# Page tiles regrouped as quarters of four pages, scales turned by VectorE, late pages gathered by GpSimd, weights and values one slot earlier

## What is computed

```python
def _decompress(c_kv, w_ukv, g_kn):
    kv = jnp.einsum('btc,chd->bthd', c_kv, w_ukv)
    return _rmsnorm(kv[..., :NOPE], g_kn), kv[..., NOPE:]

def _attn_partial(qn, qp, kn, kp, v, mask):
    s = (jnp.einsum('bqhd,bkhd->bhqk', qn, kn) + jnp.einsum('bqhr,bkr->bhqk', qp, kp)).astype(jnp.float32) * SCALE
...
    m = jnp.max(s, axis=-1)
    e = jnp.exp(s - m[..., None])
    return m, jnp.sum(e, axis=-1), jnp.einsum('bhqk,bkhd->bhqd', e, v.astype(jnp.float32))

    def step(carry, phys):
        c_blk = cache_ckv[layer, phys]
        kp_blk = cache_kpe[layer, phys]
        kn_blk, v_blk = _decompress(c_blk, w_ukv, g_kn)
        return _merge(carry, _attn_partial(qn, qp, kn_blk, kp_blk, v_blk, None)), None
```

## Time and profile before

| | us |
|---|---|
| median of 3 runs (lowest, highest) | 1275.35 (1275.25, 1277.68) |
| the profiled execution | 1276.86 |
| its span, first to last instruction | 1275.1 |
| TensorE busy | 1202.1 |
| VectorE busy | 732.2 |
| ScalarE busy | 426.5 |
| GpSimd busy | 257.4 |

### The profile page before, as it was taken

The page is one execution under the profiler, slowest core; times in us unless marked ns, Lnnn a source line. Parts: engine busy times, 40 slices in busy tenths (PEclk is TensorE's granted clock), DMA queues, the critical chain, the costliest instruction groups (busy, mean ns, idle before and its releaser), DMA issues. The chain is left out here.

```text
span 1275.1 us, 23690 instructions
## 1 busy us (share of the span) xinstructions
PE 1202.1 (94%) x8783; PEld 661.3 (52%) x8783; DVE 732.2 (57%) x1801; ACT 426.5 (33%) x1041; POOL 257.4 (20%) x294
## 2 busy tenths in 40 slices
PE   6999999989999999999989988999999999989898
PEld 3545677745565565655434445555444444454343
DVE  4000437955667666774768787888676667430331
ACT  3000354323343333342444343333444444210310
POOL 0000134711011121234412340001323232000000
PEclk9999999999999999997999999999999999999999
DMA  6413112123232222351453226532576544101000
GB/s 219 168 55 87 35 33 67 53 59 80 66 81 67 76 73 77 84 115 42 124 143 88 76 74 171 168 80 74 153 184 172 139 122 123 50 1 38 17 21 33
DMA packets 205236, 114.45 MB, mean 90 GB/s; under 512 B 152977, under 2 KB 196433, under 8 KB 204994
## 3 DMA queue, kind: packets, MB, share of 16 engines
q1 hardware_dynamic: 198482, 96.56, 27.7%
q0 software_dynamic: 4352, 10.49, 3.3%
q10 hardware_dynamic: 2288, 5.89, 1.3%
HBM read 75.79 MB, written 4.07 MB: 63 GB/s over the span
## 5 line engine op out<-in xcount | busy, mean ns | idle before, releaser
L563 PE MATMUL PS<-wk,c_T 128*128 128x512 f32 x1024 | 494.5, 612 | 13.5 <-DVE c_T L673 12.4
L563 PEld LDWEIGHTS PS<-wk,c_T 128*128 128x128 f32 x1024 | 180.3, 193 | 207.8 <-issue 162.8
L686 DVE TENSOR_REDUCE ssq<-PS 128x8 f32<-128x512 f32 x256 | 176.3, 689 | 169.7 <-ACT PS L609 156.8
L609 ACT ACTIVATE PS<-PS 128x512 f32<-128x512 f32 x256 | 150.3, 587 | 271.8 <-PE PS L563 245.0
L1557 PE MATMUL PS<-xnT,w_ring 128*128 128x276 f32 x416 | 101.0, 400 | 0.0
L1395 PE MATMUL PS<-w_ring,xnT 128*128 128x424 f32 x256 | 96.4, 534 | 0.9 <-DVE xnT L1041 0.9
L673 DVE STREAM_TRANSPOSE c_T<-blocks 128x512 f32<-128x512 f32 x126 | 88.3, 701 | 3.7 <-DMA blocks<-c_ring 3.2
L1557 PEld LDWEIGHTS PS<-xnT,w_ring 128*128 128x128 f32 x416 | 77.8, 190 | 20.6 <-issue 4.1
L489 POOL DMA_INDIRECT c_ring<-in_cache_ckv,token_rows x48 | 45.3, 944 | 182.1 <-PE PS L547 174.8
L480 POOL DMA_INDIRECT r_ring<-in_cache_kpe,group_rows x64 | 62.0, 969 | 92.3 <-DVE r_T L681 68.0
L1395 PEld LDWEIGHTS PS<-w_ring,xnT 128*128 128x128 f32 x256 | 48.8, 194 | 45.5 <-issue 45.4
(11 more groups left out here) (535 smaller groups left out, 1725.3 us busy)
## 6 DMA issues: line engine op xcount, KB each, us to landing
blocks<-c_ring SPq DMA_DIRECT2D x504, 64.0 KB
c_ring<-in_cache_ckv SPq DMA_DIRECT2D x208, 128.0 KB, 2.2
w_ring<-in_w_in SPq DMA_DIRECT2D x4, 1696.0 KB, 12.4
w_ring<-in_w_in SPq DMA_DIRECT2D x9, 512.0 KB, 5.1
w_o<-in_w_out SPq DMA_DIRECT2D x8, 512.0 KB, 4.9
w_g<-in_w_ple_gate SPq DMA_DIRECT2D x8, 512.0 KB
xn<-in_x_prompt SPq DMA_DIRECT2D x4, 512.0 KB, 10.9
w_ring<-in_w_in SPq DMA_DIRECT2D x2, 1024.0 KB, 6.1
```

The source lines that it names most:

```text
L563: mm = pe.matmul(PS[:, NORM[v % 2], :], c_T[:, u % 2, k, t * P:(t + 1) * P], wk[:, k], start=(k == 0), stop=(k == 1))
L609: nc.scalar.activation(PS[:, NORM[v % 2], :], PS[:, NORM[v % 2], :], ACT.Square).then_inc(no_sb, 1)
L686: dve.tensor_reduce(ssq[:, u % 2, t * H:(t + 1) * H], PS[:, NORM[v % 2], :].rearrange("p (h c) -> p h c", h=H), AX.X, ALU.add).then_inc(re ...
```

## The change

- **Tiles.** The tile of a slot is no longer one page but one quarter (32 tokens) of all four pages, on 4 x 32 partitions. Tokens stand in c_ring so that partition 4g+s holds token 32s+g (the source of L441 is rearranged, and so is the constant "token" for the gathers). L673 writes each half of c_T (two pages) to columns in all four tiles, so that the norms of slot 0 wait for both halves (lo_sb and hi_sb). The dots read c_T in four pieces of 32 columns.
- **Scales.** With this layout a 32 x 32 block transpose by VectorE puts each scale where its score is: scale_T takes the place of rep, L538 and the PSUM copy of the scales go. VectorE reads the scores from PSUM itself, and ScalarE's copy L604 goes.
- **Late pages.** From step 40 on GpSimd gathers all four pages. SyncE then issues only the block DMAs for those steps and no longer waits there for vv_ps.
- **Order.** TensorE: values of u-2 in slot 0 instead of slot 1, weights turned in slot 3 for u-1 instead of slot 0 for u-2. ScalarE: weights of u-1 in slot 2 instead of 3, its copy of the turned weights in slot 3 instead of the next slot 0. VectorE: merge in slot 0 instead of 1, score in slot 1 instead of 2, the halves of the next c_T in slots 2 and 3 instead of 3 and the next 0. SyncE's block DMAs are due a slot earlier.

```diff
-    parts += [("lane", s % 32), ("token", s)]
+    parts += [("lane", s % 32), ("token", s % 4 * 32 + s // 4)]
...
-                    for x in range(GT // 2 if gathered(u) else GT)]
+                    for x in range(0 if gathered(u) else GT)]
...
-                                  io["cache_ckv"][bass.ds(number, 1)].rearrange("o p c -> (o p) c")
+                                  io["cache_ckv"][bass.ds(number, 1)].rearrange("o (s g) c -> (o g) s c", s=GT)
...
-            if half == 1 and gathered(u):
-                nc.sync.wait_ge(late_in[u % 2], 32 * ((u - GATHERED) // 2 + 1))
+            if gathered(u):
+                nc.sync.wait_ge(late_in[u % 2], 64 * ((u - GATHERED) // 2 + 1))
...
-                if u >= RING:
+                if u >= RING and not gathered(u):
                     sp.wait_ge(vv_ps, u - RING + 1)
...
-                    for x in (2, 3):
+                    for x in range(GT):
...
             def dots(u):
                 pe.wait_ge(tn_sb, u + 1)
-                if u >= 1:
-                    pe.wait_ge(hi_sb, u)
...
-                                       c_T[:, u % 2, k, t * P:(t + 1) * P], start=(k == 0), stop=(k == 1))
+                                       c_T[:, u % 2, k, :].rearrange("d (q t i) -> d t q i", q=GT, t=GT)[:, t],
+                                       start=(k == 0), stop=(k == 1))
...
-                pe.transpose(PS[:, MISC, at_t], rep[:], ident).then_inc(scale_ps, 1)
...
+            def turn_weights(u):
+                pe.wait_ge(eq_sb, u + 1)
                 if u >= 1:
                     pe.wait_ge(acc_sb, u)
...
                         pe.wait_ge(lo_sb, u)
-                if t == 2 and u >= 1:
-                    pe.wait_ge(hi_sb, u)
+                        pe.wait_ge(hi_sb, u)
...
                 if t == 0 and u >= 2:
-                    turn_weights(u - 2)
+                    values(u - 2)
                 if t == 1:
                     dots(u)
-                    if u >= 2:
-                        values(u - 2)
-                if t == 2 and u >= 1:
-                    turn_scale(u - 1)
+                if t == 3 and u >= 1:
+                    turn_weights(u - 1)
                 norms(u, t)
...
+                if t == 2 and u >= 1:
+                    weights(u - 1)
                 if t == 3 and u >= 1:
-                    weights(u - 1)
+                    turned_weights(u - 1)
                 square(u, t)
...
-                dve.transpose(c_T[:, u % 2, :, 2 * half * P:2 * (half + 1) * P].rearrange("d x (t s p) -> d s t x p", t=2, s=GT),
+                dve.transpose(c_T[:, u % 2].rearrange("d x (s t g) -> d s t x g", s=GT, t=GT)[:, :, 2 * half:2 * half + 2],
...
-                dve.tensor_tensor(rep[:].rearrange("p (x t) -> p x t", t=TS),
-                                  y.rearrange("p (x o) -> p x o", o=1).to_broadcast(wide),
-                                  tmp.rearrange("p (x o) -> p x o", o=1).to_broadcast(wide), ALU.mult).then_inc(scale_sb, 1)
+                LA(dve.tensor_tensor(tmp, y, tmp, ALU.mult))
+                LA(dve.transpose(scale_T[:], tmp.rearrange("p (x o) -> p x o", o=1).to_broadcast([P, GT * H, TS])))
...
                 dve.wait_ge(rp_ps, min(u + 2, NSTEP))
-                dve.wait_ge(np_sb, u + 1)
-                dve.wait_ge(scale_ps, u + 1)
-                LA(dve.tensor_tensor(sc, sc, PS[:, MISC, at_t], ALU.mult))
+                if u >= 2:
+                    dve.wait_ge(eq_sb, u - 1)
+                LA(dve.tensor_tensor(sc, PS[:, TURN, at + P:at + 2 * P], scale_T[:], ALU.mult))
...
                 if t == 0:
+                    if u >= 2:
+                        merge(u - 2)
                     if u >= 1:
-                        turned_blocks(u, 1)
                         scales(u - 1)
-                if t == 1 and u >= 2:
-                    merge(u - 2)
-                if t == 2 and u >= 1:
+                if t == 1 and u >= 1:
                     score(u - 1)
-                if t == 3 and ahead:
-                    turned_blocks(u + 1, 0)
+                if t >= 2 and ahead:
+                    turned_blocks(u + 1, t - 2)
                 reduce(u, t)
...
-        on_sp = Stream(pages_sp(), lambda slot: 4 if slot <= PREP_SLOTS else min(2 * NSTEP, (slot + 6) // GT + (slot + 3) // GT + 2))
+        on_sp = Stream(pages_sp(), lambda slot: 4 if slot <= PREP_SLOTS else min(2 * NSTEP, (slot + 6) // GT + (slot + 4) // GT + 2))
```

More of the change, by code:

```diff
@@ L252, in build @@
         score_s = place("score_s", [P, 2, P])
-        rep = place("rep", [P, GT * QH])
+        scale_T = place("scale_T", [P, P])
         ew_q = place("ew_q", [P, P])
@@ L411, in build @@
         NFIRST = CONST["lnscale"][0] + 1
-        (slot_taken, k_ps, k_sb, tn_sb, rp_ps, no_ps, no_sb, red_sb,
-         ri_sb, scale_sb, scale_ps, np_sb, top_sb, al_sb, eq_sb, ew_ps, ew_sb, vv_ps, acc_sb, dve_a) = kept_sems(*(
-            "slot_taken k_ps k_sb tn_sb rp_ps no_ps no_sb red_sb "
-            "ri_sb scale_sb scale_ps np_sb top_sb al_sb eq_sb ew_ps ew_sb vv_ps acc_sb dve_a").split())
+        (k_ps, k_sb, tn_sb, rp_ps, no_ps, no_sb, red_sb,
+         ri_sb, top_sb, al_sb, eq_sb, ew_ps, ew_sb, vv_ps, acc_sb, dve_a) = kept_sems(*(
+            "k_ps k_sb tn_sb rp_ps no_ps no_sb red_sb "
+            "ri_sb top_sb al_sb eq_sb ew_ps ew_sb vv_ps acc_sb dve_a").split())
         c_in = [kept_sems(*(f"c_in{half}{x}" for x in range(RING))) for half in "ab"]
@@ L498, in pages_requested, with by_quarter @@
             return min(NSTEP, slot // GT + R_RING) + max(0, min(NSTEP, (slot + 6) // GT + 1) - GATHERED)
-        def by_token(k):
-            return (c_T[:, 0, k, :].rearrange("d (t s p) -> d t s p", t=GT, s=GT),
-                    PS[:, TURN, :].rearrange("d (t p s) -> d t s p", t=GT, s=GT))
+        def by_quarter(k):
+            return (c_T[:, 0, k, :].rearrange("d (s t g) -> d t s g", s=GT, t=GT),
+                    PS[:, TURN, :].rearrange("d (t g s) -> d t s g", s=GT, t=GT))
         def pages_pe():
@@ L597, in turned_first @@
                 act.wait_ge(k_ps, 1)
-                nc.scalar.copy(*by_token(0)).then_inc(k_sb, 1)
-            def dotted(u):
-                act.wait_ge(rp_ps, u + 1)
-                if u >= 2:
-                    act.wait_ge(eq_sb, u - 1)
-                nc.scalar.copy(score_s[:, u % 2, :], PS[:, TURN, u % 2 * 2 * P + P:u % 2 * 2 * P + 2 * P]).then_inc(np_sb, 1)
+                nc.scalar.copy(*by_quarter(0)).then_inc(k_sb, 1)
             def square(u, t):
@@ L680, in turned_r @@
                     dve.wait_ge(rp_ps, u)
-                dve.transpose(r_T[:], r_ring[:, u % R_RING, :]).then_inc(tn_sb, 1)
+                dve.transpose(r_T[:].rearrange("d (g s) -> d s g", s=GT),
+                              r_ring[:, u % R_RING, :].rearrange("d (s g) -> d s g", s=GT)).then_inc(tn_sb, 1)
             def reduce(u, t):
@@ L1217, in gather_rows @@
                     V(ins)
-                    late = [a.rearrange("p (j b x) -> p j b x", b=BS, x=GT)[:, :, GATHERED // STEPS:, 2:4] for a in (token_rows[:], pages[:])]
+                    late = [a.rearrange("p (j b x) -> p j b x", b=BS, x=GT)[:, :, GATHERED // STEPS:, :] for a in (token_rows[:], pages[:])]
                     dve.tensor_scalar(*late, float(P), con("token"), ALU.mult, ALU.add)
```

22 lines of the change are left out of this document (4 added, 18 removed).

## The result

The changed kernel takes 1368.01 us (median, 1366.29 to 1369.23), the kernel before 1275.8 us beside it: a ratio of 1.072, 95% interval 1.071 to 1.074. It is slower by 92 us where 1260 us, 1.2% faster, was forecast. The profiled execution of the changed kernel has a span of 1364.9 us, 89.8 more than before.

What follows compares the result with a forecast made beforehand. SyncE's in-order DMA queue was taken to bound the late steps. Terms -13.7 - 4 - 1 + 0 + 2.6 + 1 = -15.1 us from 1276.86 gave 1261.8, less 1.5 for the median: about 1260 us, range 1248 to 1275.

Steps and rivals of the forecast that it cites:

- What bounds the kernel before: Late steps: SyncE's in-order queue of page and block DMAs, 9.26 us round without free time, sets the pace.
- Late steps: 21 late steps fall from 9.15 to 8.5 us each, a gain of 13.7 us (3.2 to 15.5).
- TensorE's new order: Late steps: values, norms, dots, then remaining norms and weights' turn sum to 8.41 us; 8.5 taken (8.41 to 9.0).
- The supply: Late pages: gathers land 7.8 us after the values start, so supply allows a 7.2 us step (6.3 to 9.4).
- The score: VectorE's 1.07 us score, moved to slot 1, ends before that slot's sum can start: nothing in late steps.
- Waits of the dots and for acc: TensorE's waits outside the late stage: -4 us ahead of the dots (0 to -8.3), -1 us for acc (0 to -1.6).
- Scales and the early stages: VectorE's small product and block transpose cost +1 us (0 to 5); TensorE's own time in steps 1 to 33 nets 0.
- Beside the prompt's attention: ScalarE's weights, now in slot 2, lengthen eight waits for the attention's exponentials by 0.33 us: +2.6 us (0 to +3.3).
- E: Rival: VectorE holds up GpSimd's writing of gather orders, late steps take 10.0 us, 1292 us in all; chance 0.03.
- B: Rival: supply stays the pace, for example gathers landing 2 us later; late step 9.15 us, 1274 us; chance 0.10.
- C: Rival: the score in slot 1 delays VectorE's other work, on which TensorE waits in chains; 1283 us; chance 0.10.

Runs made afterwards that it cites:

- two_orders: The changed kernel, with values and merge behind the dots in slot 1 up to step 40, dots ahead of values in slot 0 from step 41: 1274.7 us, ratio 0.998.
- gather_waits_dots: The changed kernel, with GpSimd's late gathers for step u also waiting until the dots of step u-2 are done: 1297.8 us.
- two_gathers: The changed kernel, but from step 40 on SyncE brings pages 0 and 1 and GpSimd gathers only pages 2 and 3: 1300.6 us.
- before_gather_at_dots: The kernel before, with GpSimd's two late gathers of step u held from step 40 until the first norms of step u-1 are done: 1307.5 us.

## Why the prediction was wrong

**What bounds the kernel before: right.** Once the hold is out and pages are gathered, many late steps fall to 8.72 us; with SyncE bringing half (mean 9.68) or all (10.48) they don't.

**Late steps: wrong, +78.2 us instead of -13.7.** The failing step is in the paragraph on TensorE's new order. It summed the products as if only their issue counted, and took from the earlier trace rows how fast a signal follows, without asking what ran beside. In the earlier trace rows the values start at 964.15 and the gathers at 965.07, so behind the dots of 963.47. The paragraph on the supply itself computed that a gather starts 0.92 us behind the start of the values; with 0.54 us of values and norms of 1.82 us between the start of the values and the dots, that puts it 1.44 us ahead of the dots (measured: 1.55). The number was there, but was not set beside the dots. What it cost: the dots' signal came after 3.7 to 5.8 us instead of 0.91. The size of TensorE's own step was nearly right: 8.41 worked out, 8.5 taken, 8.72 measured, 0.2 us short.

**The supply: too hopeful.** It was to allow 7.2 us. In two_orders, without any hold, it still made eight late steps 9.1 to 9.8 us. The mis-sized term is the landing of the gathers. The sum had all four landed 7.8 us after the start of the values, so 6.9 us after the first gather started; in two_orders SyncE could start the block transfers after 6.4 to 7.2 us in most steps, but only after 7.6 to 8.2 us ahead of six of the eight long ones:

```profile
936.20 0.94 POOL L489 DMA_INDIRECT c_ring<-in_cache_ckv,token_rows  x1 [3.64 <-PE PS L542]
...
944.44 5.36 SPq L452 DMA_DIRECT2D blocks<-c_ring  x8
```

With a semaphore for each half they start 5.6 us after the first gather (6.6 in one step), and the long steps but one are gone.

**The score: wrong.** "Nothing in late steps" rested on the dots' signal at 0.9 us. VectorE idles 4.24 us ahead of the score in the step shown, and the turn of the weights two slots on has no room for that: 2.84 us of idling and 1.70 us at the lower clock, which no rival contained.

**Waits of the dots and for acc: right in kind.** 8.7 us became 0.4 us. **Scales and the early stages: not settled.** Up to step 33 the change is 3.4 us ahead, and -4, -1 and +1 say -4; but kernels alike up to there differ by as much, so the agreement may be luck. At step 22 it was 11.0 us ahead in these two traces; why it gave 7.6 of them back is open. So is what makes the rest behind step 63 3.4 us longer.

**Beside the prompt's attention: right, undersized.** The wait for the exponentials is 1.04 us at its regular place, "about 1 us instead of 0.70". Steps 33 to 37 grew by 0.55 us each, not 0.33. Steps 38 to 40 were not seen as different: +8.9 us, gone in gather_waits_dots.

**The rivals.** E was nearest, gathers hurting a late step, but by the wrong way: it let VectorE slow the gathers. In the changed kernel they did not slow at all (80 of them in the late stage, mean 948 ns), nor in any run above (means of 945 to 951 ns). The rule that a VectorE operation in a two-port mode locks GpSimd out (the Trainium skill, SBUF — State Buffer, section SBUF: two separate sides) never showed, and it says nothing of TensorE's signals.

```profile
L488 POOL DMA_INDIRECT c_ring<-in_cache_ckv,token_rows x80 | 75.8, 948 | 159.8 <-PE PS L541 141.5 <-issue 18.3
```

B's mechanism, gathers that land later than assumed, is real and cost 0.3 us a step once the hold was gone (9.02 against 8.76). C's chains didn't show: between 280 and 760 us TensorE waits 12.6 us for VectorE in the change and 13.5 before.

## What to carry to other kernels

When a wait that starts a DMA is fed by an instruction that the change moves, look at what the DMA will then run beside, not only at whether it arrives in time. Moving the values by one slot moved 6 us of gathers onto the one burst whose signal everything else waits for; the order of two calls removed the hold. Then look for the next bound: here a semaphore for each half of the data turned a tie into a gain of 0.6%.

## What the runs showed of the hardware

TensorE's completion signals are late when GpSimd's indirect DMAs are under way while a burst of small products (the 12 dots issued in 0.8 us, or the attention's) is issued. Instead of 0.91 us the dots' signal takes 3.7 to 5.8 us with five gathers in a row, 1.7 to 3.6 with three in two_gathers, and up to 3.6 with two gathers of rotary keys alone (early steps). The products behind the burst are issued on time, but their signals come only with those held. In the change and in two_gathers they come 1.8 to 2.3 us after the start of the last gather of the row in most steps and about 0.7 us after it in three; in before_gather_at_dots no such rule holds. In the late steps of all runs, gathers that begin 0.83 us or more behind the first dot, gathers beside norms of 128x512 alone, and SyncE's transfers of the same pages hold nothing. What in the chip holds them isn't shown by any run, nor whether the results are late or only the signals.

The idling of 2.84 us in a held step was followed by norms at a granted clock of 0.50, 3.68 us for four products instead of 1.98; before, with waits of 0.26 us, the late stage had no such stretch.
